# Results of the embedding stage's last three blocks in another part of the buffer, and the last norm of the output projection behind the first gate-up unit

## The chip, the cores and the metric

The program runs on all 8 cores of one Trainium2 chip. The cores do not talk to each other: each takes one prompt of 2048 tokens and 128 sample tokens through the whole layer. The metric is the device time of the slowest core in microseconds (us). A core's TensorE (PE) multiplies, VectorE (DVE) and ScalarE (ACT) do the elementwise work, GpSimd (POOL) issues the weight loads and SyncE (SP) issues the other transfers.

## What is computed

One layer of a decoder, in bf16 matmuls and float32 elementwise work. Cut to what matters:

```
h = x + 0.5 * rmsnorm(swiglu(rmsnorm(x) , W1))                 # FFN 1
n = rmsnorm(h) ; b,c,h_a,u,v = n @ W_in                        # mixer
y_a = b * causal_conv3(c * h_a) ; y_b = u * (tril(W_s) @ rmsnorm(v) + b_s)
h = h + rmsnorm(concat(rmsnorm(y_a), rmsnorm(y_b)) @ W_out)    # output projection
h = h + 0.5 * rmsnorm(swiglu(rmsnorm(h), W2))                  # FFN 2
h = h + rmsnorm(sigmoid(h @ W_pg) * (p @ W_pp))                # embedding stage
swiglu(x) = (silu(x @ W_gate) * (x @ W_up)) @ W_down
```

The model width is 1024, the hidden width of an FFN 2816 (22 column blocks of 128).

## The kernel before

A core works in two **passes**. Pass 0 has nine blocks of 128 tokens in three tiles of 384, pass 1 has eight blocks in two tiles of 512. Each pass runs these stages: gate-up of FFN 1 (`gu_stage`), down projection (`tok_stage`), `mixer`, output projection (`tok_stage` again, with lag 3), gate-up of FFN 2, down projection, and the embedding stage (`ple`). There is no scheduler: each engine executes its instructions in the order in which this Python code issues them, and waits on semaphores where `wait` puts them.

**A gate-up unit** (`gu_unit`) is two hidden blocks j of one tile: for each, 8 matmuls of the gate and 8 of the up part into a PSUM bank each. ACT takes Silu of the gate bank into one of two `sg` buffers, DVE multiplies the up bank with it into `hmid` (the product). There are eight banks, taken in rotation, so the ninth group of matmuls needs the first bank back. The first three weight slots (`heads`) are used on all tiles in turn: units (0,0), (1,0), (2,0) of tile 0, then (0,1), (1,1), (2,1) of tile 1, and so on. A hook can be issued inside a unit: `(s, ti): (jj, fn)` issues fn behind product jj of unit (s, ti).

**The output projection** makes, for each block b, one pair of banks. ACT takes the square sum, Ln and Exp of it (`post_stat`), DVE updates `h` (`post_apply`). The norm ahead of FFN 2 lags a block behind (`pend` and `pre_fn`): ACT squares `h` into one of two `nbr` buffers, then Ln and Exp, then DVE scales it into `nbr`, and SP issues a transpose DMA into `nT` (`pre_mid`, `pre`, `turn`). Two transposes are never in flight at once. A buffer's next Square waits until its transpose has landed. The last block's norm is issued at the end of `tok_stage`, ahead of everything of the gate-up stage. Then SP issues two gain loads, POOL the load of p (`pT`), and `pay_owed` lets POOL issue the weight fills that `hold_fills` held back, once the last transpose has landed.

**The buffer `big`** holds, one after the other, `hmid` of a pass, the mixer's work, and in the embedding stage the results `gb(b)` of its blocks. Counted in float32 columns, `hmid` block j lies at 576 j. Before the change `gb(b)` of blocks 0 to 3 lies at 1024 b, of blocks 4 and 5 in `zsc`, and blocks 6, 7 and 8 use the places of blocks 0, 1 and 2 again. The first x tile of pass 1 lies at 8192 to 12287, the second at 4096 to 8191. The embedding stage works in groups of three blocks. It also normalises the first x tile of pass 1 (`x_apply`) in group 1; the second is squared and normalised from the hooks `next_square` and `next_mid` in pass 1's gate-up.

Each result is stored to HBM by SP (`store`, event `out_ev[b]`). `gb_guard` lets a block's Sigmoid wait for what was in its place; `guard1` does the same for the products of pass 1's first gate-up.

Of the kernel before, what the change touches and what calls it, by code (L numbers as in the profile page):

```python
# [26 lines left out]
G1POST, GMPRE, GMPOST, G2PRE, G2POST, GPLE = range(6)  # L27
NGAIN = 6
# [92 lines left out]
def build_program():  # L121
    nc = bass.Bass("TRN2", target_bir_lowering=False)
# [9 lines left out]
    pT_d = din("pT", [128, 2, NTOK])  # L132
# [19 lines left out]
    POOL = Eng(nc, nc.gpsimd, "pool")  # L152

    h_t = nc.alloc_sbuf_tensor("h", [128, 9, D], F32)
    nT_t = nc.alloc_sbuf_tensor("nT", [128, 8, WMAX], BF16)
# [3 lines left out]
    zsc_t = nc.alloc_sbuf_tensor("zsc", [128, 2, D], F32)  # L159
# [13 lines left out]
    bigf = big_t[:].bitcast(F32)  # L173
# [5 lines left out]
        return hmid[:, j0:j0 + 8, b * 128:(b + 1) * 128]  # L179

    def gb(b):
        i = b % 6
        return zsc_t[:, i - 4, :] if i >= 4 else bigf[:, 1024 * i:1024 * (i + 1)]

    ps = [nc.alloc_psum_tensor("ps%d" % i, [128, 1024], F32) for i in range(4)]
    banks = [Bank(ps[i // 2][:, 512 * (i % 2):512 * (i % 2) + 512]) for i in range(8)]
# [73 lines left out]
    def pay_owed(wait, limit=2 * NFILL):  # L260
        POOL.wait(wait)
        wr["limit"] = limit
        n, wr["owed"] = wr["owed"], 0
        for _ in range(n):
            issue_next()
# [17 lines left out]
    def gain_load(i, wait=None):  # L283
        if i >= 2 * NGAIN:
            return
        SP.wait(wait)
        gain_ev[i] = gain_sem[i % 3].add(nc.sync.dma_start(
            out=gain_t[:, i % 3, :], in_=gain_d[i % NGAIN:i % NGAIN + 1, :].broadcast_to([128, D])))
# [22 lines left out]
    nT_ev = {}  # L311
# [141 lines left out]
    def gu_stage(P, heads, guard, hooks=None, order=None):  # L453
        hooks = hooks or {}
        hd = [next_fill() for _ in range(heads)]
        evl = None
        nt = len(P.tiles)
        for s, ti in order or [(s, ti) for ti in range(nt) for s in range(heads)]:
            f, fev = hd[s]
            evl = gu_unit(P, f, fev, 2 * s, ti, guard, hooks.get((s, ti)))  # L460
            if ti == nt - 1:
                release(f, evl)
        for s in range(heads, NFF // 2):
            f, fev = next_fill()
            for ti in range(nt):
                evl = gu_unit(P, f, fev, 2 * s, ti, guard, hooks.get((s, ti)))
            release(f, evl)


    xn_ev = {}  # L470
# [89 lines left out]
    def tok_stage(P, nk, nfl, lhs, wait, gpost, c, lag, j0, pre_fn, hooks=None):  # L560
        fl = [next_fill() for _ in range(nfl)]
        pend = None
        for b in range(P.nb):
            last = b == P.nb - 1
            pair, ev = proj_block(P, b, nk, lambda k, b=b: lhs(b, k), 4, fl, wait(b), last)
            if hooks and b in hooks:
                hooks[b](ev)
            st = post_stat(b, pair, ev, c, j0)
            e = post_apply(b, pair, st, gpost)
            if lag == 1:  # L570
                pre_fn(b, ev)
            else:
                if pend is not None:
                    pre_fn(*pend)
                pend = (b, ev)
        if pend is not None:
            pre_fn(*pend)
        return e


    vo_sem = DmaSem(nc, "vo")
# [389 lines left out]
    h_free = {}  # L971

    def gb_guard(b):
        return [guards["zsc"] if b % 6 >= 4 else None, out_ev.get(b - 6) if b >= 6 else None]


    first = x_stat(PASSES[0], 0, x_square(PASSES[0], 0))
# [33 lines left out]
    for P in PASSES:  # L1011
        base = P.idx * NGAIN
        N = PASSES[P.idx + 1] if P.idx == 0 else None

        def guard1(j, P=P):
            if P.idx == 0:
                return None
            lo, hi = j * 576 // 1024, (j * 576 + 575) // 1024
            evs = [out_ev.get(x + 6 if x < 3 else x) for x in range(lo, hi + 1) if x < 4]
            if hi >= 4:  # L1020
                evs += [xn_ev[1, 1][-1], xn_ev[1, 0][-1]]
            return evs

        def guard_none(j):
            return None

        if P.idx == 0:
            gu_stage(P, 2, guard1, {(1, 0): (1, start_square), (1, 1): (0, start_mid), (2, 0): (0, start_loads),
                                    (8, 0): (0, late_consts)},
                     [(0, 0), (0, 1), (1, 0), (1, 1), (0, 2), (1, 2)])  # L1030
        else:
            gu_stage(P, 3, guard1, {(0, 0): (1, next_square), (1, 0): (1, next_mid)})
        xn_ev.clear()
        def pre_mid(gi):
            def f(b, ev_d):
                dst, ev_t = turn_buffer()
                last_pre["ev"] = e = pre(b, gi, dst, [ev_d, ev_t])
                turn(b, dst, e)
            return f

        last_pre = {"ev": None}
        nT_ev.clear()
        hold_fills()
        tok_stage(P, NFF, 6, lambda b, k: hmid[:, k, b * 128:(b + 1) * 128], lambda b, P=P: [hm[P.tile_of(b)]],
                  base + G1POST, 4.0, 1, 14, pre_mid(base + GMPRE))
        pay_owed([nT_ev[P.nb - 1]])
        gain_load(base + G2PRE, [last_pre["ev"]])
        gain_load(base + G2POST, [last_pre["ev"]])

        norm_ev, tail, vo_last = mixer(P)  # L1050
        ACT.wait(vo_last)
        nT_ev.clear()
        tok_stage(P, 8, 2, lambda b, k: nT_t[:, k, b * 128:(b + 1) * 128], lambda b: [norm_ev[b]],
                  base + GMPOST, 1.0, 3, 0, pre_mid(base + G2PRE), {0: tail})
        gain_load(base + GPLE, [last_pre["ev"]])
        gain_load(base + NGAIN + G1POST, [last_pre["ev"]])

        POOL.wait(vo_last, last_pre["ev"])
        w = P.tiles[-1][0] + P.tiles[-1][1]
        pT_ev = None  # L1060
        for i, r0 in enumerate(sorted(set([P.rows[0]] + ([P.rows[8]] if P.nb == 9 else [])))):
            n = 1024 if i == 0 else 128
            pT_ev = pt_sem.add(nc.gpsimd.dma_start(out=pT_v[:, :, i * 1024:i * 1024 + n], in_=pT_d[:, :, r0:r0 + n]))
        pay_owed([nT_ev[P.nb - 1]])
        gu_stage(P, 3, guard_none)
        hold_fills(1)

        def next_x(ev):
            xt_load(PASSES[1], 0, 1, [ev])

        def cast(b, ev_d):
            dst, ev_t = turn_buffer()
            turn(b, dst, copy_v([h_ev[b], ev_t], dst, h_t[:, b, :].rearrange("p (k s) -> p k s", k=8)))

        nT_ev.clear()
        tok_stage(P, NFF, 6, lambda b, k: hmid[:, k, b * 128:(b + 1) * 128], lambda b, P=P: [hm[P.tile_of(b)]],
                  base + G2POST, 4.0, 1, 0, cast, {8: next_x} if N is not None else None)
        guards["zsc"] = h_ev[P.nb - 1]
        groups = [[0, 1, 2], [3, 4, 5], [6, 7, 8]] if P.nb == 9 else [[0, 1, 2], [3, 4, 5], [6, 7]]
        ple(P, N, base, pT_ev, groups)  # L1080
        if N is not None:
            pay_owed([xt_ev[1, 1]])
        zfree[0], zfree[1] = out_ev[4], out_ev[5]
# [101 lines left out]
```

How the kernel before makes its waits and increments, by code:

```python
    def wait(self, *evs):  # L62
        best = {}
        for ev in _flat(evs, []):
            if ev.key not in best or best[ev.key].val < ev.val:
                best[ev.key] = ev
        for ev in best.values():
            if self.seen.get(ev.key, 0) >= ev.val:
                continue
            self.e.wait_ge(ev.sem, ev.val)
            self.seen[ev.key] = ev.val
            if _COLLECT is not None and ev.idx is not None:
                _COLLECT.add((ev.key, ev.idx))
# [1 line left out]
    def mark(self, ins):  # L75
        self.idx += 1
        if _USED is not None and (self.name, self.idx) not in _USED:
            return Ev(self.sem, self.n, self.name, self.idx)
        self.n += 1
        ins.then_inc(self.sem, 1)
        return Ev(self.sem, self.n, self.name, self.idx)
# [8 lines left out]
    def add(self, ins):  # L90
        self.n += 16
        ins.then_inc(self.sem, 16)
        return Ev(self.sem, self.n, self.name)
```

## Time and profile before

| quantity | before |
|---|---|
| time, median of 3 runs | 1333.33 us (1333.08 to 1335.34) |
| time of the profiled execution | 1332.94 us |
| its span on the slowest core (core 2) | 1331.8 us |
| spans of the eight cores | 1326.5 to 1331.8 us |
| PE busy in the span | 1290.0 us (97%) |
| mean granted TensorE clock, by core | 0.989 to 0.993 |
| a weight transfer of 512 KB, from issue to landing (median) | 15.1 us |
| table loads on ACT (core 2) | 25 |

The profile's rows come from one profiled execution. A timeline row has the start in us from the span's start, the length in us, the engine and line, the operation as output<-inputs with the shape, and how many instructions it merges. In brackets stands the idle time ahead of it and what ended it. Some matmul records are missing, so a merged row can show 63 where 64 ran.

### The profile page before, as it was taken

How to read it: one execution, taken by the hardware profiler on the slowest of the kernel's cores; microseconds unless marked ns; L12 is line 12 of the kernel's file. 1: busy time of each engine (PE TensorE's matmuls, PEld its weight loads, DVE VectorE, ACT ScalarE, POOL GpSimd, SP SyncE). 2: the span in 40 equal slices, each digit the busy share in tenths (PEclk: the TensorE clock that was granted, in tenths of full speed). 3: DMA queues.
4: the chain of work that ended last, by engine and by line, in shares of the span. 5: the costliest groups of instructions: out<-in, count | busy, mean ns of one | idle time of the engine just before them, and what ended most of it. 6: DMA issues, size and time to landing. Idle time of an engine off the chain costs nothing.

```text
span 1331.8 us, 18723 instructions; the slowest of 8 cores (1326.5 to 1331.8 us)
## 1 busy us (share of the span) xinstructions
PE 1290.0 (97%) x6734; PEld 651.8 (49%) x6816; DVE 524.1 (39%) x694; ACT 411.3 (31%) x862; POOL 94.7 (7%) x185
## 2 busy tenths in 40 slices
PE   8999999999999999999998999999999999999995
PEld 6566664455545666654443344444444444444442
DVE  3222222447696222213266321223477922122237
ACT  3311112344465111111166211123334721111136
POOL 2110000001001100000001100000010011000000
PEclk9999999999999999999999899999999999999998
DMA  8999322129725963231289994332297299333123
GB/s 186 201 208 207 65 48 48 24 39 178 123 49 108 168 110 64 48 72 25 48 176 257 215 182 79 58 62 32 48 179 130 56 144 175 69 63 58 32 40 126
DMA packets 88906, 139.89 MB, mean 105 GB/s; under 512 B 58352, under 2 KB 58608, under 8 KB 88432
## 3 DMA queue, kind: packets, MB, share of 16 engines
q0 software_dynamic: 25296, 90.25, 41.1%
q1 hardware_dynamic: 63520, 48.43, 13.5%
q8 instruction: 57, 0.93, 0.3%
q14 instruction: 33, 0.27, 0.1%
HBM read 206.03 MB, written 9.51 MB: 162 GB/s over the span
## 4 chain that ended last, share of the span: by engine, by line
PE 85%; DVE 5%; ACT 4%; DMA 3%; issue 3%; SPq 0%; ACTq 0%; DVEq 0%
PE ps L212 56%; PE ps L557 24%; PE ps L546 3%; DVE nT L221 1%; DMA y<-big 1%; DMA nT<-nbr 1%; ACT big L217 1%; DMA h<-xT 1%; DVE big L225 1%; DVE big L221 1%; ACT sg L217 1%; DVE nbr L221 1%; ACT L217 1%; PE ps L711 1%; ACT nbr L217 1%
## 5 line engine op out<-in xcount | busy, mean ns | idle before, releaser
L212 PE MATMUL ps<-nT,ring 128*128 128x384 bf16 (+1 forms) x4127 | 776.6, 349 | 16.4 <-DVE nT L221 7.9
L212 PEld LDWEIGHTS ps<-nT,ring 128*128 128x128 bf16 x4160 | 407.9, 98 | 381.4 <-issue 29.4
L225 DVE TENSOR_TENSOR big<-ps,sg 128x384 bf16<-128x384 f32 (+1 forms) x220 | 134.0, 611 | 489.3 <-PE ps L212 469.8
L557 PE MATMUL ps<-ring,big 128*128 128x512 bf16 x1291 | 283.7, 379 | 1.5
L217 ACT ACTIVATE sg<-ps 128x384 f32<-128x384 f32 (+1 forms) x237 | 127.0, 537 | 500.9 <-PE ps L212 490.3
L557 PEld LDWEIGHTS ps<-ring,big 128*128 128x128 bf16 x1320 | 129.2, 98 | 155.5
L253 POOL DMA_DIRECT2D ring<-w x170 | 90.2, 539 | 1066.7 <-PE ps L212 461.5
L217 ACT ACTIVATE big<-ps 128x1024 bf16<-128x1024 f32 (+4 forms) x89 | 75.4, 862 | 226.3 <-PE ps L557 195.2
L225 DVE TENSOR_TENSOR zsc<-ps,gains 128x1024 f32<-128x1024 f32 x51 | 62.3, 1222 | 180.2 <-ACT big L217 180.1
L557 PE MATMUL ps<-ring,nT 128*128 128x512 bf16 x470 | 104.9, 379 | 2.1 <-DVE big L225 1.4
L557 PEld LDWEIGHTS ps<-ring,nT 128*128 128x128 bf16 x480 | 46.8, 98 | 58.3 <-issue 2.5
L221 DVE SCALAR_TENSOR_TENSOR h<-zsc,st,h 128x1024 f32<-128x1024 f32 x51 | 65.5, 1285 | 11.1 <-DVE zsc L225 6.7
L225 DVE TENSOR_TENSOR big<-ps,big 128x384 f32<-128x384 f32 (+3 forms) x78 | 50.3, 678 | 39.8 <-PE ps L212 20.4
L221 DVE SCALAR_TENSOR_TENSOR nbr<-h,st,gains 128x1024 bf16<-128x1024 f32 x34 | 43.6, 1282 | 36.4 <-ACT st L217 36.4
L217 ACT ACTIVATE nbr<-h 128x1024 bf16<-128x1024 f32 x34 | 35.9, 1057 | 50.4 <-DVE h L221 41.9
L217 ACT ACTIVATE st<-st 128x1 f32<-128x1 f32 x205 | 41.7, 203 | 18.7 <-ACT st L217 0.7
L546 PE MATMUL ps<-ring,big 128*128 128x512 bf16 x175 | 38.6, 379 | 0.1
L217 ACT ACTIVATE big<-big 128x384 bf16<-128x384 f32 (+3 forms) x46 | 26.2, 605 | 38.0 <-DVE big L225 38.0
L217 ACT ACT_TABLE_LOAD x25 | 32.1, 1283 | 13.0 <-PE ps L212 6.0
L212 PE MATMUL ps<-ring,nT 128*128 128x512 bf16 x131 | 29.4, 379 | 0.3
L546 PEld LDWEIGHTS ps<-ring,big 128*128 128x128 bf16 x176 | 17.2, 98 | 20.8
L221 DVE SCALAR_TENSOR_TENSOR big<-big,gc 128x384 f32<-128x384 f32 (+3 forms) x48 | 24.8, 590 | 0.0
(73 smaller groups left out, 363.5 us busy)
## 6 DMA issues: line engine op xcount, KB each, us to landing
ring<-w POOLq DMA_DIRECT2D x170, 512.0 KB, 15.1
h<-x SPq DMA_DIRECT2D x17, 512.0 KB, 30.2
gains<-gain SPq DMA_DIRECT2D x12, 512.0 KB, 9.2
y<-big SPq DMA_DIRECT2D x12, 512.0 KB, 10.8
big<-xT SPq DMA_DIRECT2D x2, 2048.0 KB, 13.8
y<-zsc SPq DMA_DIRECT2D x4, 512.0 KB, 6.2
h<-xT SPq DMA_DIRECT2D x4, 384.0 KB, 5.9
h<-xT SPq DMA_DIRECT2D x2, 768.0 KB, 10.7
```

Of the source, the lines that this page charges most:

```text
L212: ins = nc.tensor.matmul(out_ap, l, r, start=(i == 0), stop=(i == n - 1))
L217: return ACT.mark(nc.scalar.activation(**kw))
L221: return DVE.mark(nc.vector.scalar_tensor_tensor(out=out, in0=in0, scalar=scalar, in1=in1, op0=op0, op1=op1))
L225: return DVE.mark(nc.vector.tensor_tensor(out=out, in0=in0, in1=in1, op=op))
L253: nc.gpsimd.dma_start(out=ring_t[:, s, o:o + HALF], in_=w_d[f % NFILL, :, o:o + HALF])))
L546: ins = nc.tensor.matmul(o.t, lhs(k), sv[:, k % per, half * 512:half * 512 + 512], start=(k == 0), stop=(k == nk - 1))
L557: ins = nc.tensor.matmul(o.t, lhs(k), sv, start=(k == 0), stop=(k == nk - 1))
L711: ins = nc.tensor.matmul(bank.t[:, 0:w], ones_t[:], sq[i][:, 0:w], start=(c == 0), stop=(c == 3))
```

## The change

Two things are changed. First, `gb(b)` of blocks 6, 7 and 8 lies at 8192, 9216 and 10240, in the room of pass 1's first x tile. Their Sigmoid waits until that tile has been normalised, where it waited for the stores of blocks 0, 1 and 2. The products of pass 1's first gate-up wait for the stores of whatever lies in their place now: blocks 0 to 3 for the first places, blocks 6 to 8 from place 8192 on. Second, `tok_stage` returns its pending block instead of issuing its norm. After the output projection that norm, and all that came behind it (two gain loads, the load of p, the held fills), is issued as a hook behind the second product of unit (0,0).

```diff
@@ gb @@
-        i = b % 6
-        return zsc_t[:, i - 4, :] if i >= 4 else bigf[:, 1024 * i:1024 * (i + 1)]
+        if b in (4, 5):
+            return zsc_t[:, b - 4, :]
+        o = 1024 * b if b < 4 else 8192 + 1024 * (b - 6)
+        return bigf[:, o:o + 1024]
@@ tok_stage @@
-        if pend is not None:
-            pre_fn(*pend)
-        return e
+        return pend
@@ gb_guard @@
-        return [guards["zsc"] if b % 6 >= 4 else None, out_ev.get(b - 6) if b >= 6 else None]
+        if b in (4, 5):
+            return [guards["zsc"]]
+        return [xn_ev[1, 0][-1]] if b >= 6 and (1, 0) in xn_ev else []
@@ guard1 @@
-            evs = [out_ev.get(x + 6 if x < 3 else x) for x in range(lo, hi + 1) if x < 4]
-            if hi >= 4:
-                evs += [xn_ev[1, 1][-1], xn_ev[1, 0][-1]]
+            evs = []
+            for x in range(lo, hi + 1):
+                if x < 4:
+                    evs.append(out_ev[x])
+                elif x < 8:
+                    evs.append(xn_ev[1, 1][-1])
+                else:
+                    evs += [xn_ev[1, 0][-1], out_ev[x - 2] if x < 11 else None]
@@ the pass loop @@
-        tok_stage(P, 8, 2, lambda b, k: nT_t[:, k, b * 128:(b + 1) * 128], lambda b: [norm_ev[b]],
-                  base + GMPOST, 1.0, 3, 0, pre_mid(base + G2PRE), {0: tail})
-        gain_load(base + GPLE, [last_pre["ev"]])
-        gain_load(base + NGAIN + G1POST, [last_pre["ev"]])
-
-        POOL.wait(vo_last, last_pre["ev"])
...
-        pay_owed([nT_ev[P.nb - 1]])
-        gu_stage(P, 3, guard_none)
+        pre_ffn2 = pre_mid(base + G2PRE)
+        pend = tok_stage(P, 8, 2, lambda b, k: nT_t[:, k, b * 128:(b + 1) * 128], lambda b: [norm_ev[b]],
+                         base + GMPOST, 1.0, 3, 0, pre_ffn2, {0: tail})
+        ple_in = {}
+
+        def last_norm(P=P):
+            pre_ffn2(*pend)
+            gain_load(base + GPLE, [last_pre["ev"]])
+            gain_load(base + NGAIN + G1POST, [last_pre["ev"]])
+            POOL.wait(vo_last, last_pre["ev"])
...
+            pay_owed([nT_ev[P.nb - 1]])
+
+        gu_stage(P, 3, guard_none, {(0, 0): (1, last_norm)})
```

What stands on DVE where pass 0 ends and pass 1 begins: the last block of the embedding stage, then the products of pass 1's first gate-up (`big<-ps,sg`), then the normalising of the second x tile (`nT<-big,gc,ps`). y6 is the store of block 6. Before:

```order
L221 SCALAR_TENSOR_TENSOR big<-big,st,gains 128x1024 [waits sem_act]
L225 TENSOR_TENSOR big<-big,h 128x1024 [waits sem_dve]
L225 TENSOR_TENSOR big<-ps,sg 128x512 [waits sem_act,sem_pe,y6]
L225 TENSOR_TENSOR big<-ps,sg 128x512 [waits sem_act,sem_pe,y7]
L225 TENSOR_TENSOR big<-ps,sg 128x512 [waits sem_act,sem_pe]
L225 TENSOR_TENSOR big<-ps,sg 128x512 [waits sem_act,sem_pe,y8]
L221 SCALAR_TENSOR_TENSOR nT<-big,gc,ps 128x512 [waits sem_act]
L221 SCALAR_TENSOR_TENSOR nT<-big,gc,ps 128x512 x7
```

The same place after:

```order
L223 SCALAR_TENSOR_TENSOR big<-big,st,gains 128x1024 [waits sem_act]
L227 TENSOR_TENSOR big<-big,h 128x1024 [waits sem_dve]
L227 TENSOR_TENSOR big<-ps,sg 128x512 [waits sem_act,sem_pe,y0]
L227 TENSOR_TENSOR big<-ps,sg 128x512 [waits sem_act,sem_pe,y1]
L227 TENSOR_TENSOR big<-ps,sg 128x512 [waits sem_act,sem_pe]
L227 TENSOR_TENSOR big<-ps,sg 128x512 [waits sem_act,sem_pe,y2]
L223 SCALAR_TENSOR_TENSOR nT<-big,gc,ps 128x512 [waits sem_act]
L223 SCALAR_TENSOR_TENSOR nT<-big,gc,ps 128x512 x7
```

The instructions and their order are the same; the stores waited for are those of blocks 0, 1 and 2 where they were those of 6, 7 and 8.

What stands on ACT at the end of pass 1's output projection: `nbr,st<-h` is the Square of a block's norm, `st<-st` its Ln and Exp, `sg<-ps` a Silu of the gate-up stage; t0 and t1 are transposes. Before:

```order
L217 ACTIVATE st<-st 128x1 [waits sem_act] x2
L217 ACTIVATE nbr,st<-h 128x1024 [waits sem_dve,t1]
L217 ACTIVATE st<-st 128x1 [waits sem_act] x2
L217 ACTIVATE nbr,st<-h 128x1024 [waits sem_dve,t0]
L217 ACTIVATE st<-st 128x1 [waits sem_act] x2
L217 ACTIVATE sg<-ps 128x512 [waits sem_pe] x2
L217 ACTIVATE sg<-ps 128x512 [waits sem_pe,sem_dve] x42
```

The same place after:

```order
L219 ACTIVATE st<-st 128x1 [waits sem_act] x2
L219 ACTIVATE nbr,st<-h 128x1024 [waits sem_dve,t1]
L219 ACTIVATE st<-st 128x1 [waits sem_act] x2
L219 ACTIVATE sg<-ps 128x512 [waits sem_pe] x2
L219 ACTIVATE nbr,st<-h 128x1024 [waits sem_dve,t0]
L219 ACTIVATE st<-st 128x1 [waits sem_act] x2
L219 ACTIVATE sg<-ps 128x512 [waits sem_pe,sem_dve] x42
```

Two Silus moved ahead of the last block's Square, Ln and Exp. Pass 0 has the same move at its output projection. Table loads of ACT are not listed here; they come where the function changes between Silu and Ln or Exp.

## Rows read from the trace of the kernel before

**Rows 1.** The page: PE's share, and the chain that ended last by engine.

```profile
PE 1290.0 (97%) x6734; PEld 651.8 (49%) x6816; DVE 524.1 (39%) x694; ACT 411.3 (31%) x862; POOL 94.7 (7%) x185
...
PE 85%; DVE 5%; ACT 4%; DMA 3%; issue 3%; SPq 0%; ACTq 0%; DVEq 0%
```

**Rows 2.** Waits: who waited for whom, total us, times, longest.

```profile
DVE big L225 <- DMA y<-big: 13.5, 3, 5.6
...
PE ps L212 <- DVE nT L221: 7.9, 11, 3.7
```

**Rows 3.** Timeline of PE where pass 0 ends and pass 1 begins.

```profile
709.22 13.97 PE L212 MATMUL ps<-nT,ring 128*128 128x512 bf16 x63
723.03 1.89 PE L500 MATMUL ps<-nT,ones 128*128 128x512 bf16 x7
727.83 8.75 PE L212 MATMUL ps<-nT,ring 128*128 128x512 bf16 x32 [2.91 <-DVE big L225]
738.28 0.38 PE L212 MATMUL ps<-nT,ring 128*128 128x512 bf16 x1 [1.70 <-DVE nT L221]
```

**Rows 4.** Timeline of DVE in the same stretch.

```profile
720.10 1.22 DVE L225 TENSOR_TENSOR big<-big,h 128x1024 f32<-128x1024 f32 x1
726.89 0.69 DVE L225 TENSOR_TENSOR big<-ps,sg 128x512 bf16<-128x512 f32 x1 [5.57 <-DMA y<-big]
...
737.40 5.34 DVE L221 SCALAR_TENSOR_TENSOR nT<-big,gc,ps 128x512 bf16<-128x512 f32 x8
...
760.47 0.69 DVE L225 TENSOR_TENSOR big<-ps,sg 128x512 bf16<-128x512 f32 x1 [2.76 <-PE ps L212]
```

**Rows 5.** Timeline of ACT in the same stretch.

```profile
718.12 1.09 ACT L217 ACTIVATE sg<-ps 128x512 f32<-128x512 f32 x2
719.10 3.89 ACT L217 ACTIVATE nT<-big 128x1024 bf16<-128x1024 f32 x4
...
733.05 1.28 ACT L217 ACT_TABLE_LOAD   x1
734.34 1.25 ACT L217 ACTIVATE ps<-ps 128x512 f32<-128x512 f32 x2
```

**Rows 6.** Windows: busy time by engine, then granted clock, DMA share, GB/s.

```profile
736.00:745.00 9.00, 6.37 (x15) 1.62 (x15) 7.15 (x11) 2.69 (x4) 1.06 (x2) 0.68 1.03 176
```

**Rows 7.** Timeline of PE, pass 0, first gate-up units of FFN 2.

```profile
406.79 10.56 PE L212 MATMUL ps<-nT,ring 128*128 128x384 bf16 x64
419.17 41.11 PE L212 MATMUL ps<-nT,ring 128*128 128x384 bf16 x252 [1.82 <-ACT sg L217]
```

**Rows 8.** Timeline of ACT, pass 0: Ln and Exp of block 7's norm.

```profile
412.84 0.50 ACT L217 ACTIVATE st<-st 128x1 f32<-128x1 f32 x2
```

**Rows 9.** Timeline of ACT, pass 1: blocks 6 and 7 of the same norm.

```profile
1059.84 0.50 ACT L217 ACTIVATE st<-st 128x1 f32<-128x1 f32 x2
1062.00 1.06 ACT L217 ACTIVATE nbr<-h 128x1024 bf16<-128x1024 f32 x1 [1.66 <-DMA nT<-nbr]
```

**Rows 10.** Core 2, pass 1: PE's gate-up; the last two transposes; time to landing.

```profile
1054.51 40.74 PE L212 MATMUL ps<-nT,ring 128*128 128x512 bf16 x185 [1.15 <-DMA nT<-nbr]
...
1062.66 4.35 SPq L325 DMA_TRANSPOSE nT<-nbr  x2
...
DMA to landing us min/median/max: 3.0/3.0/7.6
```

**Rows 11.** Core 7, the same three.

```profile
1054.34 25.84 PE L212 MATMUL ps<-nT,ring 128*128 128x512 bf16 x119 [1.15 <-DMA nT<-nbr]
...
1062.51 4.34 SPq L325 DMA_TRANSPOSE nT<-nbr  x2
...
DMA to landing us min/median/max: 3.0/5.9/8.7
```

**Rows 12.** Core 7, start of pass 1: PE's first row, DVE's fifth product of tile 1.

```profile
708.74 13.97 PE L212 MATMUL ps<-nT,ring 128*128 128x512 bf16 x64
...
760.31 0.69 DVE L225 TENSOR_TENSOR big<-ps,sg 128x512 bf16<-128x512 f32 x1 [2.76 <-PE ps L212]
```

More of the change, by code:

```diff
@@ L1052, in build_program @@
         nT_ev.clear()
-        tok_stage(P, 8, 2, lambda b, k: nT_t[:, k, b * 128:(b + 1) * 128], lambda b: [norm_ev[b]],
-                  base + GMPOST, 1.0, 3, 0, pre_mid(base + G2PRE), {0: tail})
-        gain_load(base + GPLE, [last_pre["ev"]])
-        gain_load(base + NGAIN + G1POST, [last_pre["ev"]])
-        POOL.wait(vo_last, last_pre["ev"])
[L1059 to L1063, printed above, removed]
-        pay_owed([nT_ev[P.nb - 1]])
-        gu_stage(P, 3, guard_none)
+        pre_ffn2 = pre_mid(base + G2PRE)
[7 more added lines that the diff above has]
+            POOL.wait(vo_last, last_pre["ev"])
+            for i, r0 in enumerate(sorted(set([P.rows[0]] + ([P.rows[8]] if P.nb == 9 else [])))):
+                n = 1024 if i == 0 else 128
+                ple_in["ev"] = pt_sem.add(nc.gpsimd.dma_start(out=pT_v[:, :, i * 1024:i * 1024 + n],
+                                                              in_=pT_d[:, :, r0:r0 + n]))
+            pay_owed([nT_ev[P.nb - 1]])
+        gu_stage(P, 3, guard_none, {(0, 0): (1, last_norm)})
+        pT_ev = ple_in["ev"]
         hold_fills(1)
```

## The prediction

> **What bounds the kernel now.** I read the page first. PE is busy for 97% of the span and makes 85% of the chain that ended last [rows 1], so a time can only be won where PE stands still or runs at a lower clock. The list of waits says where that is. PE's largest wait is 7.9 us for DVE's normalising into nT, and DVE's one wait on a transfer in a PE-bound stretch is 13.5 us for stores `y<-big`, in three pieces [rows 2]. The timelines put both at the same place, the start of pass 1. I then read the other two places that the change touches: the output projections of both passes.
>
> **Part 1, the boundary of the passes.** In the first gate-up of pass 1 the first product on DVE could start when DVE is done with the last embedding block (720.10 + 1.22 = 721.3), but starts at 726.89, after 5.57 us of waiting for a store [rows 4]; the second and third pieces of the 13.5 us follow behind the next products. The products free PSUM banks and `sg` buffers, so PE stops for 2.91 us after the statistics matmuls, and again ahead of tile 1, where nT is normalised only from 737.40 on, one k every 0.67 us, each matmul waiting for one [rows 3, 4]. The standing PE also loses its clock: 0.68 of full speed in 736 to 745 [rows 6].
>
> What would PE do without any of this? 64 matmuls took 13.97 us, a last one included that takes 0.38, so the pace is (13.97 - 0.38) / 63 = 0.2157 us [rows 3]. The fifth product of tile 1, at 760.47 [rows 4], follows the 184th matmul from 709.22 (64, then 8 of the statistics, 32 of unit (2,0), and 80 of tile 1). Unhindered, that one ends at 709.22 + 183 x 0.2157 + 0.38 = 749.1, and the product starts about 0.1 later. So at most 760.47 - 749.2 = **11.3 us** are to be won here, clock included.
>
> Is all of it won? The stores now waited for, of blocks 0 to 2, were issued in group 0 of the embedding stage, more than 20 us earlier, so that wait is gone. What is late next is the way over ACT and DVE to the second x tile. ACT does its two Silus at 718.12 and the four squares until 719.10 + 3.89 = 723.0 [rows 5]. Then two more Silus (1.1, to 724.1, their buffers free since the products of 721.3 to 722.7), a table load of 1.28 (to 725.4), Ln and Exp of 1.25 (to 726.7) [rows 5]. The statistics matmuls end at 723.03 + 1.89 = 724.9 [rows 3], before that. DVE then needs 5.34 for the eight k [rows 4], so it ends at 732.1. PE does unit (2,0) from 724.8 to 731.7 (32 x 0.2157) and wants k = 7 of tile 1 at 731.7 + 7 x 0.2157 = 733.2. The margin is 1.1 us, so nothing of the wait comes back. If the chain were later than this, every us beyond 1.1 would be lost. The weights are there: PE waits for none in this stretch, and their loads go on as before. Moving the blocks' results costs nothing else. The Sigmoid of block 6 waits for the normalising of the first x tile instead of for a store, and DVE does that normalising before it does the products of group 1, whose statistics stand ahead of this Sigmoid on ACT. In pass 1 nothing of this kind was on the way.
>
> **Part 2, pass 0's output projection.** PE does the 64 matmuls of two units from 406.79 at a pace of (10.56 - 0.33) / 63 = 0.1624, could begin the ninth group at 417.18, and begins at 419.17, released by a Silu [rows 7]. That Silu stood behind block 8's norm, which waited for its buffer. After the change it stands behind block 7's Exp, which ends at 412.84 + 0.50 = 413.3 [rows 8], plus a table load of 1.28: it starts at 414.6, and its bank is free at 415.1, two us before it is wanted. **2.0 us** are won. The last norm then needs a table load more, is 1.5 us later, and the third Silu follows at about 420.0. Its bank is wanted at 417.2 + 32 x 0.1624 = 422.4, so PE does not stop again. Block 8 belongs to tile 2, which PE reaches after twelve j of 2.6 us, at 438; its transpose is issued at about 420.6 and, even with the 8.7 us of the slowest one shown [rows 11], is there by 429.3.
>
> **Part 3, pass 1's output projection.** Here PE did not wait for a Silu, so nothing is won. But the norm of block 7 gets later, and block 7 belongs to tile 1. Before: Square at 1062.00 [rows 9]. After: Exp of block 6 ends at 1059.84 + 0.50 = 1060.3, table load 1.28, two Silus 1.1, Square at 1062.7, 0.7 later; then one more table load of 1.28 ahead of Ln. Together the transpose is issued 2.0 us later. On core 2 the last transpose was issued at 1062.66 + 4.35 - 1.24 = 1065.8 and took 7.6 us (the load of p is issued with it, and stays with it), so it landed at 1073.4. PE wants tile 1 at 1054.51 + 96 x 0.2157 = 1075.2 [rows 10]. After: 1075.4, and 0.1 for PE to start: PE stands for **0.3 us**. On core 7 the same reckoning gives a landing at 1065.6 + 8.7 = 1074.3 against a want of 1075.05 [rows 11], so 1.3 us late afterwards: 1.3 us, 1.4 with the start. Cores with 1326 to 1330 us have larger margins or do not matter. The held fills start 2 us later too; the first of them is used after three heads and one more slot, at 1054.5 + 256 x 0.2157 = 1109.7, more than 30 us after its issue, and such a transfer takes 15 us.
>
> Here a rule speaks against the change. The rows show a switch of table as 1.28 us and nothing more: the load starts at 733.05 as the Silu ends, and Ln starts at 734.34 [rows 5]. The Trainium skill, "ScalarE: Activation LUTs", section "What ACT_TABLE_LOAD costs", adds a drain of about 1.38 us to each load of 1.28. By it the two switches ahead of the last norm would cost 2.8 us more. The sum below takes the row.
>
> **The sum.** Core 2: 1331.8 - 11.3 - 2.0 + 0.3 = 1318.8. Core 7 had 1331.6, and its stretch at the boundary, counted in the same way, holds 760.31 - 708.74 - 40.0 = 11.6 [rows 12]: 1331.6 - 11.6 - 2.0 + 1.4 = 1319.4. The slowest core ends at about 1319.2, that is 12.6 less. The profiled execution took 1332.94, the median is 0.4 above it; 1333.33 - 12.6 = **1320.7 us**.
>
> **Rivals.**
> (a) The boundary keeps a part: the way over squares, table load, Ln, Exp and eight normalising steps is 2 to 5 us longer than I built it, so that 1 to 4 us of the 11.3 stay, or PE's clock falls there all the same. For: it has six links and a margin of 1.1. Against: each link has a row. Time 1322 to 1325.
> (b) Each switch between Silu and Ln costs more than its row while other work is in ACT's pipe, 1.4 us a switch. Then block 7's transpose lands 2.8 us later still and PE stands 3.1 us (core 2) to 4.2 (core 7): 1323.5. Against: the rows show back-to-back starts on both sides of the load. This is the page's case, too.
> (c) The change does not do what it says at the boundary: another transfer, such as the stores of blocks 1 and 2, holds the products. These would have to be 20 us and more in flight; the longest wait for stores shown is for ones issued at 716 to 721. Then only part 2 remains: 1331.7.
> (d) The other side: in pass 1 the transpose of block 7, now issued as PE is in the middle of tile 0, lands far later than 7.6 us, because its slot among the load of p and the gain load is worse. It costs nothing up to 1.8 us of delay on core 2 and then us for us. To make the kernel slower by 0.2% it has to be 1.8 + 13.3 + 2.7 = 18 us later than before; 2 are worked out. Its price is then 1336 or more.
>
> **How the numbers follow.** The forecast as summed 0.80 (1319.0 to 1322.3 by the spread of the cores' terms: 11.0 to 11.9 at the boundary, 0 to 1.4 in part 3, and the spread of the runs), (a) 0.12, (b) 0.04, (c) 0.03, (d) 0.01. The range reaches over (b) and most of (a): 1319.0 to 1324.0. A measurement of this kernel tells about 0.2%, 2.7 us, from no change. Faster by more: 0.96; within: 0.03, from (c); slower: 0.01, from (d).
>
> **What would show it.** DVE's first product of pass 1 starts at the end of the last embedding block, with no idle time charged to `y<-big`; the row of 2.91 us and the seven of 0.28 us on PE are gone, and the clock is 1.00 in every window of the boundary. In pass 0 PE's row after 64 matmuls of FFN 2's gate-up has no wait for ACT. In pass 1 a new row of PE, 96 matmuls after the start of that gate-up, waits 0 to 1.5 us for `nT<-nbr`. ACT has two table loads more in each pass, 29 for 25. I am wrong if PE still stands at the start of tile 1 in pass 1's first gate-up, or if the new wait exceeds 2 us.

## The result, and the profile after

| quantity | before | after |
|---|---|---|
| time, median | 1333.9 us (4 runs, 1333.1 to 1335.3) | 1320.0 us (4 runs, 1319.7 to 1321.7) |
| profiled execution | 1332.94 us | 1319.69 us |
| its span, slowest core (core 2 in both) | 1331.8 us | 1318.6 us |
| spans of the eight cores | 1326.5 to 1331.8 us | 1314.7 to 1318.6 us |
| sum of PE's waits (core 2) | 22.2 us | 14.8 us |

The ratio is 0.9897, with a 95% interval of 0.988 to 0.9914. The medians here and below leave out the runs in which the cores of a die show a lower granted clock and a longer time (of after one in five, 1433.9 us).

The page of after: its span, the busy times, the chain that ended last, and the group of table loads.

```profile
span 1318.6 us, 18725 instructions; the slowest of 8 cores (1314.7 to 1318.6 us)
...
PE 1284.3 (97%) x6734; PEld 651.3 (49%) x6816; DVE 524.0 (40%) x694; ACT 415.6 (32%) x866; POOL 94.7 (7%) x185
...
PE 90%; DVE 3%; ACT 3%; issue 2%; DMA 2%; SPq 0%; ACTq 0%; DVEq 0%; POOLq 0%
...
L219 ACT ACT_TABLE_LOAD x29 | 37.2, 1283 | 13.6 <-PE ps L214 5.4
```

PE's busy time fell by 5.7 us with the same number of matmuls as in [rows 1]: that is clock won back. The rest of the 13.2 us is standing time. PE's part of the chain rose from 85% to 90%. The table loads are 29, as worked out.

PE's waits in after (who waited for whom, total us, times, longest):

```profile
PE ps L214 <- DMA ring<-w: 3.3, 1, 3.3
PE ps L214 <- DVE nT L223: 1.9, 7, 0.7
```

The first is PE's wait for the first weights at the start of the kernel. The second was 7.9 us in [rows 2], but less of that lay at the boundary than it seems. In the execution before, this row of PE's timeline stands at the kernel's start:

```profile
22.12 20.04 PE L212 MATMUL ps<-nT,ring 128*128 128x384 bf16 x112 [3.71 <-DVE nT L221]
```

This start wait (3.71 us) is still there after, 3.34 us at 21.84, now put down to the weights. Another 1.9 us, at 46 to 50 us, are the 1.9 of the second row. Only 2.3 us of the 7.9 were at the boundary, and these are gone. DVE's 13.5 us for `y<-big` is gone from the list too.

**The boundary of the passes.** PE of core 2, the stretch of [rows 3]:

```profile
707.09 13.97 PE L214 MATMUL ps<-nT,ring 128*128 128x512 bf16 x63
720.90 1.89 PE L502 MATMUL ps<-nT,ones 128*128 128x512 bf16 x7
722.62 42.68 PE L214 MATMUL ps<-nT,ring 128*128 128x512 bf16 x193
```

DVE in the same stretch, to be laid beside [rows 4]:

```profile
717.96 1.23 DVE L227 TENSOR_TENSOR big<-big,h 128x1024 f32<-128x1024 f32 x1
719.10 1.28 DVE L227 TENSOR_TENSOR big<-ps,sg 128x512 bf16<-128x512 f32 x2
721.51 1.29 DVE L227 TENSOR_TENSOR big<-ps,sg 128x512 bf16<-128x512 f32 x2 [1.13 <-ACT sg L219]
725.52 5.36 DVE L223 SCALAR_TENSOR_TENSOR nT<-big,gc,ps 128x512 bf16<-128x512 f32 x8 [2.72 <-ACT ps L219]
...
747.07 0.69 DVE L227 TENSOR_TENSOR big<-ps,sg 128x512 bf16<-128x512 f32 x1 [2.76 <-PE ps L214]
```

PE runs through without one idle stretch. The first product follows the last embedding block at once. The fifth product of tile 1 comes 747.07 - 707.09 = 39.98 us after PE's first matmul of the pass, where it took 51.25 before. The granted clock is full where it was 0.68 [rows 6] (columns: stretch, length, busy time of PE, weight load, DVE, ACT, POOL, then clock, DMA share, GB/s):

```profile
727.00:736.00 9.00, 8.95 (x42) 4.05 (x42) 5.77 (x9) 2.12 (x4) 1.06 (x2) 1.00 1.00 190
736.00:745.00 9.00, 8.95 (x42) 4.12 (x42) 2.08 (x3) 1.19 (x2) 1.06 (x2) 1.00 1.03 198
```

ACT in that stretch, beside [rows 5]:

```profile
720.75 1.08 ACT L219 ACTIVATE sg<-ps 128x512 f32<-128x512 f32 x2
722.87 1.28 ACT L219 ACT_TABLE_LOAD   x1 [1.04 <-PE ps L502]
724.16 1.26 ACT L219 ACTIVATE ps<-ps 128x512 f32<-128x512 f32 x2
```

Here one thing is not as worked out. The table load does not begin when the Silus end (721.8) but only at 722.87, after PE's statistics matmuls, for which the Ln behind it waits.

**Pass 0's output projection.** PE's timeline, where [rows 7] had a stop of 1.82 us:

```profile
406.62 23.56 PE L214 MATMUL ps<-nT,ring 128*128 128x384 bf16 x144
```

ACT's timeline there, to be laid beside [rows 8]:

```profile
413.20 1.28 ACT L219 ACT_TABLE_LOAD   x1
414.49 0.87 ACT L219 ACTIVATE sg<-ps 128x384 f32<-128x384 f32 x2
415.25 1.06 ACT L219 ACTIVATE nbr<-h 128x1024 bf16<-128x1024 f32 x1
...
419.58 0.87 ACT L219 ACTIVATE sg<-ps 128x384 f32<-128x384 f32 x2
```

From there to the first matmul of pass 1 the core took 709.22 - 406.79 = 302.43 us before and 707.09 - 406.62 = 300.47 after: 1.96 us less.

**Pass 1's output projection.** PE's timeline on core 2, the stretch of [rows 10]:

```profile
1041.12 39.23 PE L214 MATMUL ps<-nT,ring 128*128 128x512 bf16 x178 [1.16 <-DMA nT<-nbr]
```

ACT's, the stretch of [rows 9]:

```profile
1047.11 1.28 ACT L219 ACT_TABLE_LOAD   x1
1048.41 1.08 ACT L219 ACTIVATE sg<-ps 128x512 f32<-128x512 f32 x2
1049.38 1.06 ACT L219 ACTIVATE nbr<-h 128x1024 bf16<-128x1024 f32 x1
...
1050.60 1.28 ACT L219 ACT_TABLE_LOAD   x1
1051.90 0.50 ACT L219 ACTIVATE st<-st 128x1 f32<-128x1 f32 x2
```

DVE's row of block 7's scaling:

```profile
1052.50 1.28 DVE L223 SCALAR_TENSOR_TENSOR nbr<-h,st,gains 128x1024 bf16<-128x1024 f32 x1 [2.03 <-ACT st L219]
```

SyncE's row of block 7's transpose (start, length and number), and its time to landing:

```profile
L327 SPq DMA_TRANSPOSE nT<-nbr x1: 1232/1232/1232, 1053.9 to 1053.9; - x1
...
DMA to landing us min/median/max: 7.3/7.3/7.3
```

The transpose lands at 1053.9 + 7.3 = 1061.2, and PE wants tile 1 at 1041.12 + 96 x 0.2157 = 1061.8. Core 2 does not wait, and in this execution neither does any other.

### The profile page after: what moved, and what is told of

Its sections match the earlier page's. It is cut to its first block, busy times and chain, and to the rows that moved or that the text cites. A ratio compares the mean times of both kernels' runs of the same rounds, so it can differ in the third digit from the quotient of the medians.

```text
span 1318.6 us, 18725 instructions; the slowest of 8 cores (1314.7 to 1318.6 us)
## 1 busy us (share of the span) xinstructions
PE 1284.3 (97%) x6734; PEld 651.3 (49%) x6816; DVE 524.0 (40%) x694; ACT 415.6 (32%) x866; POOL 94.7 (7%) x185
## 4 chain that ended last, share of the span: by engine, by line
PE 90%; DVE 3%; ACT 3%; issue 2%; DMA 2%; SPq 0%; ACTq 0%; DVEq 0%; POOLq 0%
PE ps L214 59%; PE ps L559 26%; PE ps L548 3%; DVE nT L223 1%; DMA h<-xT 1%; DVE big L223 1%; ACT sg L219 1%; ACT big L219 1%; DVE big L227 1%; ACT L219 1%; DMA ring<-w 1%; PE ps L711 1%; DMA nT<-nbr 0%; PE ps L862 0%; PE ps L807 0%
## 5 line engine op out<-in xcount | busy, mean ns | idle before, releaser
L214 PEld LDWEIGHTS ps<-nT,ring 128*128 128x128 bf16 x4160 | 407.5, 98 | 368.3 <-issue 13.5
L219 ACT ACT_TABLE_LOAD x29 | 37.2, 1283 | 13.6 <-PE ps L214 5.4
L223 DVE SCALAR_TENSOR_TENSOR nT<-big,gc,zsc 128x384 bf16<-128x384 f32 (+1 forms) x40 | 23.9, 667 | 2.2 <-ACT zsc L219 2.2
## 6 DMA issues: line engine op xcount, KB each, us to landing
ring<-w POOLq DMA_DIRECT2D x170, 512.0 KB, 14.8
```

The lines of the kernel that those rows point to most:

```text
L214: ins = nc.tensor.matmul(out_ap, l, r, start=(i == 0), stop=(i == n - 1))
L219: return ACT.mark(nc.scalar.activation(**kw))
L223: return DVE.mark(nc.vector.scalar_tensor_tensor(out=out, in0=in0, scalar=scalar, in1=in1, op0=op0, op1=op1))
```

## Experiments

Two theories stood against each other at the boundary. **Theory W:** DVE's waits for late stores cost the 11.3 us, and their way goes over PE's banks, the second x tile and the clock. **Theory P:** it is not these waits but something else that went with them, the places in the buffer or the norm's order. For the norm, theory N said that pass 0 gains 2 us and pass 1 pays 0 to 1.4 us for a later transpose. The diffs are against after.

The cores reach one and the same instruction at times that differ by some us from core to core and from execution to execution. So the table has, beside the median, the time from PE's first matmul of FFN 2's gate-up in pass 0 (406.62 on core 2 of after) to the core's end, lowest and highest of the eight cores of the profiled execution. All that the experiments touch lies in this stretch. It was 924.7 to 926.1 us before and 911.7 to 912.2 after.

| run | what | median, us | ratio to before (95%) | gate-up to end, us |
|---|---|---|---|---|
| e1_place_only | norm where it was | 1323.1 | 0.9917 (0.9901 to 0.9934) | 913.6 to 913.7 |
| e2_norm_only | places and waits of before | 1330.8 | 0.9977 (0.9966 to 0.9987) | 921.3 to 922.5 |
| e3_old_waits | places of after, waits of before as well | 1331.4 | 0.9979 (0.9966 to 0.9991) | 921.6 to 924.1 |
| e4_one_wait | only the first of these waits | 1326.6 | 0.9941 (0.9925 to 0.9958) | 914.2 to 918.7 |
| e5_norm_later | pass 1: norm one unit later | 1325.9 | 0.9939 (0.9923 to 0.9955) | 913.9 to 917.9 |
| e6_norm_pass0 | norm moved in pass 0 alone | 1321.3 | 0.9908 (0.9892 to 0.9923) | 911.6 to 912.2 |
| e7_two_copies | 3.9 us of spare work ahead of Ln | 1323.4 | 0.9928 (0.9914 to 0.9942) | 914.4 to 914.6 |
| e8_early_load | table load pulled ahead | 1320.1 | 0.9902 (0.9886 to 0.9918) | 911.6 to 912.2, one core 913.4 |
| e9_later_p_after | e5, load of p behind the transpose | 1321.3 | 0.991 (0.9894 to 0.9927) | 911.6 to 911.9 |
| e10_later_both_after | e9, gain loads behind it too | 1319.7 | 0.9898 (0.9883 to 0.9913) | 911.7 to 912.2 |
| e11_both_after | after, both loads behind, and e8 | 1319.8 | 0.9898 (0.9882 to 0.9915) | 911.6 to 912.0 |

### Each half alone

e1_place_only issues the norm ahead of the gate-up stage again:

```diff
-        gu_stage(P, 3, guard_none, {(0, 0): (1, last_norm)})
+        last_norm()
+        gu_stage(P, 3, guard_none)
```

> The changed kernel with the last norm of the output projection issued where the kernel before had it; only the place of the results of blocks 6 to 8 and the waits that follow from it are new. My theory: the 11.3 us of the boundary of the passes (waits on stores, waits on x tile 2, lower clock) are all this part's, so 11 to 11.5 us less than before, some 1322.5; PE in pass 0 waits 1.8 us for a Silu again. Rival, the two parts work together (the boundary is won only with the norm moved): well under 11 us.

The boundary took 750.78 - 710.80 = 39.98 us on the slowest core (core 7), so all of the 11.3 us is there without the norm's move. In pass 0 PE's wait was back (its timeline):

```profile
420.75 3.57 PE L214 MATMUL ps<-nT,ring 128*128 128x384 bf16 x21 [1.85 <-ACT sg L219]
```

The median is 3.1 us above after's. The wait accounts for 1.7 to 1.8 of it: from the start of the gate-up in pass 0 to the end the core took 1322.0 - 408.33 = 913.7 us, against 1318.6 - 406.62 = 912.0, and the other seven cores agree. In the profiled executions the rest, 408.33 - 406.62 = 1.7 us, is how late the slowest core came to that gate-up; of this more below.

e2_norm_only has `gb`, `gb_guard` and `guard1` of before and the norm of after:

```diff
@@ gb @@
...
+        i = b % 6
+        return zsc_t[:, i - 4, :] if i >= 4 else bigf[:, 1024 * i:1024 * (i + 1)]
...
@@ guard1 @@
...
+            evs = [out_ev.get(x + 6 if x < 3 else x) for x in range(lo, hi + 1) if x < 4]
...
```

> The kernel before with only the last norm moved behind the first gate-up unit. My theory: 2.0 us less than before (pass 0's wait of 1.8 us for a Silu goes), nothing or up to 0.5 us lost in pass 1, so some 1331.5 to 1332; the boundary of the passes is as before, with three waits on stores of 13 us in total. Rival, each switch of ACT's table costs 1.4 us more than its row: Ln of the last norm starts 2.7 us after its table load begins and pass 1 shows a wait of PE for a transpose of 2 us and more, so no gain.

It gained 3.1 us, a little more than expected. DVE waited for stores again at the boundary (6.47, 4.29 and 2.90 us on core 6), which lost 758.61 - 707.78 - 39.98 = 10.85 us. In pass 1 no core waited for the later transpose. The two halves are independent as far as this tells: what each is worth alone (10.8 and 3.1 by the medians) adds up to the whole, 13.9.

### The waits, not the places

e3_old_waits keeps every place of after and adds waits that nothing needs, for the stores of blocks 6, 7 and 8:

```diff
                 if x < 4:
                     evs.append(out_ev[x])
+                    evs.append(out_ev[x + 6] if x < 3 else None)
```

> The changed kernel, with the new places, but the products of pass 1's first gate-up wait for the stores of blocks 6, 7 and 8 as well, as they did before (nothing needs these waits now). My theory: the wait alone is the cost, so the 11.3 us come back: 2 us less than before, some 1332. Rival, the gain comes from the places (transfers or engines meeting in the same part of the buffer): most of the 11 us stays won, some 1321 to 1323.

DVE on the slowest core (core 0):

```profile
724.64 0.69 DVE L227 TENSOR_TENSOR big<-ps,sg 128x512 bf16<-128x512 f32 x1 [5.83 <-DMA y<-big]
729.52 1.29 DVE L227 TENSOR_TENSOR big<-ps,sg 128x512 bf16<-128x512 f32 x2 [4.18 <-DMA y<-big]
734.20 0.69 DVE L227 TENSOR_TENSOR big<-ps,sg 128x512 bf16<-128x512 f32 x1 [3.40 <-DMA y<-big]
...
758.83 0.69 DVE L227 TENSOR_TENSOR big<-ps,sg 128x512 bf16<-128x512 f32 x1 [2.76 <-PE ps L214]
```

This is the picture of [rows 4], and with PE's first matmul at 706.71 the fifth product came 52.1 us later, 12.1 more than in after. The median is 11.4 us above after's. On the eight cores the stretch from the gate-up to the end is 10 to 12 us longer than in after. Theory W holds, and P falls: the new places are worth nothing but the waits that they make needless.

e4_one_wait adds the first of the three waits only:

```diff
+                    evs.append(out_ev[6] if x == 0 else None)
```

> The changed kernel, but the first product of pass 1 waits for the store of block 6 too; those of blocks 7 and 8 are not waited for. My theory: product 0 starts about 5.5 us late, the banks and the second x tile follow: PE stands 2.9 us ahead of unit (2,0) and up to 1 us at tile 1, and the clock falls for some us: 4 to 5.5 us slower than the changed kernel, some 1325 to 1326. Rival, the three waits add up only by the last one (block 8), the first being covered by the banks in hand: within 1 us of the changed kernel. If the clock does not fall after 2.9 us of standing, 3 to 4 us.

DVE's timeline on the slowest core (core 4):

```profile
727.50 1.29 DVE L227 TENSOR_TENSOR big<-ps,sg 128x512 bf16<-128x512 f32 x2 [6.23 <-DMA y<-big]
```

PE's, on the same core:

```profile
728.45 36.77 PE L214 MATMUL ps<-nT,ring 128*128 128x512 bf16 x163 [3.57 <-DVE big L227]
```

One window of it, columns as above:

```profile
727.00:736.00 9.00, 7.55 (x29) 3.15 (x30) 6.49 (x10) 6.12 (x8) 0.77 (x3) 0.81 1.03 254
```

The stretch took 754.31 - 709.17 = 45.14 us, 5.16 more than in after: 3.57 of standing, and the other 1.6 of clock, which was 0.81 in the window with the end of the stop and what follows it. On this core one wait of 6.2 us on DVE thus costs 5.2; over the eight cores waits of 4.3 to 7.3 us cost 2.3 to 6.8 (by the stretch to the end, against some 911.9). With the other two waits the cost is 10 to 12. The median is 6.6 us above after's, more than the 4 to 5.5 expected; the slowest core had again come late to pass 0's gate-up (408.72 against 406.62).

### How much room the second x tile has

e7_two_copies puts two spare copies on ACT ahead of the statistics' Ln (the result is not touched):

```diff
     def next_mid():
+        e = None
+        for _ in range(2):
+            e = act([e, t_ev], out=nbr_t[:].rearrange("p i k s -> p (i k s)"), in_=XT[1, 1][:, 0:2048], func=AF.Copy)
```

> The changed kernel with 3.8 us of spare work on ACT (two copies of 2048 columns into an idle buffer) between the Silus of unit (1,0) and the Ln of the second x tile's statistics. If ACT's table load ahead of that Ln waits until the statistics are done, as the row of the changed kernel looks (load at 722.87, after 1.04 us of waiting for PE), the load moves from 722.87 to 725.7: Ln and all behind it 2.8 us later, the margin of 0.15 us at k = 7 used up, PE loses 2.7 us and maybe some clock: some 1323.5. If the margin is the 1.1 us of my prediction, PE loses 1.7 us. Rival, the way over ACT has slack that the rows do not show: no loss.

ACT's timeline on the slowest core (core 4):

```profile
723.41 3.92 ACT L219 ACTIVATE nbr<-big 128x2048 bf16<-128x2048 f32 x2
727.34 1.28 ACT L219 ACT_TABLE_LOAD   x1
```

DVE's, on the same core:

```profile
730.00 5.35 DVE L223 SCALAR_TENSOR_TENSOR nT<-big,gc,ps 128x512 bf16<-128x512 f32 x8 [5.48 <-ACT ps L219]
...
737.71 0.69 DVE L227 TENSOR_TENSOR big<-ps,sg 128x512 bf16<-128x512 f32 x1 [1.16 <-PE ps L214]
```

The first of PE's six stops there:

```profile
732.20 0.38 PE L214 MATMUL ps<-nT,ring 128*128 128x512 bf16 x1 [0.28 <-DVE nT L223]
```

The normalising started 730.00 - 708.80 = 21.20 us after PE's first matmul, against 725.52 - 707.09 = 18.43 in after: 2.77 later. The first product of tile 1 came 737.71 - 708.80 = 28.91 us after it, where after (at 733.25) took 26.16: 2.75 later. So nearly all of the delay reached PE, and every core shows it: the stretch to the end is 2.5 to 2.7 us longer than the 911.9 that is the middle of after's. With the margin of 1.1 us that the prediction gave to this way, 1.7 would have reached PE.

e8_early_load lets ACT compute one column's Ln that waits for nothing, ahead of the Ln of the statistics:

```diff
     def next_mid():
+        act([ev_ones], out=st_t[:, 15, 3:4], in_=ones_t[:, 0:1], func=AF.Ln)
```

> The changed kernel with one spare Ln of one column ahead of the statistics' Ln, which waits for nothing, so that the table load is done while PE still makes the statistics. My theory: the Ln starts 0.8 to 0.9 us earlier, the normalising of the second x tile ends 0.8 us earlier and the margin at k = 7 grows from 0.15 to 1.0 us; the time is the same as the changed kernel's, since PE does not wait there. Rival, PE does wait there on some cores: up to 0.5 us faster.

ACT's timeline on the slowest core (core 0):

```profile
721.18 1.28 ACT L219 ACT_TABLE_LOAD   x1
722.48 0.20 ACT L219 ACTIVATE st<-ones 128x1 f32<-128x1 bf16 x1
```

DVE's normalising there:

```profile
723.95 5.36 DVE L223 SCALAR_TENSOR_TENSOR nT<-big,gc,ps 128x512 bf16<-128x512 f32 x8 [1.81 <-ACT ps L219]
```

The load now lies beside the statistics matmuls, and the normalising starts 723.95 - 706.42 = 17.53 us after PE's first matmul, 0.9 earlier than in after. So the missing 0.9 us of margin was the table load behind Ln's wait. The time is after's, since PE waited for nothing there in after. In the same execution core 0 waited for block 7's transpose in pass 1 (PE's timeline):

```profile
1062.82 17.43 PE L214 MATMUL ps<-nT,ring 128*128 128x512 bf16 x80 [1.49 <-DMA nT<-nbr]
```

It had taken 9.6 us to land. The norm is issued there as in after.

### The norm in pass 1, and what makes its transpose slow

e6_norm_pass0 moves the norm in pass 0 only:

```diff
+        if P.idx == 0:
+            gu_stage(P, 3, guard_none, {(0, 0): (1, last_norm)})
+        else:
+            last_norm()
+            gu_stage(P, 3, guard_none)
```

> The changed kernel with the last norm moved in pass 0 alone; pass 1 issues it as before. My theory: the move wins nothing in pass 1 and costs nothing there either now, so the same time as the changed kernel within 0.5 us (about 1320.5 to 1321). Rival, the move helps pass 1 too (Silus earlier): up to 2 us slower than the changed kernel. Rival, it costs pass 1 up to 1.4 us on the slowest core: 1319.5.

Its median is 1.3 us above after's, with runs from 1319.9 to 1321.4 us; by these the two can't be told apart. The stretch from the gate-up to the end is sharper: 911.6 to 912.2 us, as in after. Moving the norm in pass 1 neither wins nor loses in these executions.

e5_norm_later moves it one unit further there, `(P.idx, 0)` for `(0, 0)`:

> The changed kernel with pass 1's last norm issued behind the second gate-up unit instead of the first (pass 0 as changed). My theory: the transpose is issued some 4.3 us later (Square behind the Silu of block j = 3) and lands at about 1065.5 against PE's want of tile 1 at 1061.8: PE waits 3 to 4.5 us, the kernel is that much slower than the changed one, some 1324 to 1325; that shows how near the changed kernel is to paying. Rival, the transpose has no use for its time because PE is fed by other tiles: no wait, same time.

PE's timeline on the slowest core (core 0):

```profile
1067.70 12.64 PE L214 MATMUL ps<-nT,ring 128*128 128x512 bf16 x50 [3.82 <-DMA nT<-nbr]
```

Time from issue to landing of SyncE's transposes in that stretch:

```profile
DMA to landing us min/median/max: 3.0/3.0/7.2
```

All eight cores waited, 2.0 to 4.3 us, where 3 to 4.5 were expected. The last transposes took 5.4 to 7.7 us, though the same transfer takes 3.0 elsewhere. e9_later_p_after keeps the late norm and lets POOL start the load of p only when that transpose has landed:

```diff
-            POOL.wait(vo_last, last_pre["ev"])
+            POOL.wait(vo_last, last_pre["ev"], nT_ev[P.nb - 1])
```

> The kernel of e5_norm_later (pass 1's last norm behind the second unit), but POOL issues the load of p only when the last transpose has landed, in both passes. Open: why that transpose takes 5.4 to 7.7 us where the others take 3.0. My theory: it shares the DMA engines with the load of p issued at the same moment, so it lands in 3 to 4 us now, and the wait of PE for it falls from 2.0 to 4.3 us by core to about 0 to 1: some 1321.5. Rival, the gain load that SP issues behind it is as much in its way: landing and wait stay, some 1325. Rival, the cause is outside the core (memory traffic of the other cores): landing stays at 5 to 8.

Their time to landing on the slowest core (core 7):

```profile
DMA to landing us min/median/max: 3.0/3.0/3.1
```

It was 3.0 to 3.1 us on every core, and no core's PE waited: 4.6 us of e5's 5.9 came back. e10_later_both_after lets the gain loads wait as well (the second is issued behind the first on SyncE):

```diff
-            gain_load(base + GPLE, [last_pre["ev"]])
+            gain_load(base + GPLE, [last_pre["ev"], nT_ev[P.nb - 1]])
```

> As e9_later_p_after, and SP issues the gain loads too only when the last transpose has landed. If either load holds the transpose up, it lands in 3.0 to 3.1 us on every core and PE waits for it nowhere: 1320.5 to 1321. If the cause is outside the core, 5 to 8 us stay.

The landings were 3.0 to 3.1 us again, so the gain loads add nothing to the transpose's time. The load of p is what stretches it. The median is 1.6 us below e9's, but from the gate-up of pass 0 to the end the slowest cores of the two profiled executions took the same: 1319.3 - 407.62 = 911.7 and 1318.7 - 407.05 = 911.7 us. Nothing behind that point makes the difference.

e11_both_after is the candidate for a better kernel: after, with both loads behind the transpose and the early table load of e8.

> The changed kernel (norm behind the first unit) with the load of p and the gain loads behind the last transpose's landing, and with the early table load of e8. My theory: no core can wait for block 7's rows any more (one of eight did, 1.49 us, in e8's profiled execution), the margins at the boundary are 1 us; the time is that of the changed kernel or up to 0.7 us less, 1320 to 1321. Rival, the later loads of p and of the fills are missed somewhere: slower, above 1322.

No core waits for the last transpose, which lands in 3.0 to 3.2 us, and it takes 1319.8 us, which can't be told from after's 1320.0. No kernel here beats after by what can be measured.

## Why the prediction was right, point by point

**The forecast.** 1320.7 us against 1320.0, and 12.6 less in the profiled execution against 1332.94 - 1319.69 = 13.25. (By the medians the fall is 13.9, as that of before came out at 1333.9. The 12.6 goes with an end at 1319.2, where the line for core 7 gives 1319.4.) The sum of the two gains measured on core 2, 11.27 + 1.96 = 13.23, is its whole difference of 1331.8 - 1318.6 = 13.2.

**Part 1, 11.3 us: right, and for the reason given.** The pace of 0.2157 us laid over the 184 matmuls gave the 40.0 us of the free way. After and e1 show it, and in e3 the waits take it away again. The clock's part was rightly inside that count and not added to it. One reading was off: the whole 7.9 us for `nT` were put at the boundary and seven stops of 0.28 us there, where 2.3 us and two such stops are charged on core 2. The sum did not use them. PE's standing in the stretch adds up to 2.9 + 2.3 + 0.2 = 5.4 us, so more than half of the 11.3 was clock.

**The margin of 1.1 us: wrong in size.** The normalising ended at 725.52 + 5.36 = 730.88, and PE wanted the eighth k of tile 1 at 722.62 + 39 x 0.2157 = 731.03. That leaves 0.15 us. The step that failed is "a table load of 1.28 (to 725.4)". Counted from PE's first matmul of the pass, the two Silus were to end at 14.9 us and ended at 14.7, the statistics matmuls were to end at 15.7 and did. But the load was taken to start with the Silus' end and to run beside these matmuls, and it waited for them with its Ln: Ln was worked out for 725.4 - 709.22 = 16.2 us and came at 724.16 - 707.09 = 17.1. These 0.9 us are what e8 wins back. The result was right by 0.15 us, and e7 shows what more would have cost: us for us, though without the clock. That nothing at all was lost here was in part luck.

**Part 2, 2.0 us: right.** It came as 1.96, the Silu at 414.49 (worked out: 414.6), the third one at 419.58 (420.0).

**Part 3, a loss of 0.3 to 1.4 us: wrong, it was 0.** DVE's scaling came 2.05 us later, as worked out (1052.50 - 1041.12 = 11.38 us after the gate-up's start, against 1063.84 - 1054.51 = 9.33). The step that failed is the next one: "Together the transpose is issued 2.0 us later". In the execution before, DVE was done with the scaling at 1065.1:

```profile
1063.84 1.28 DVE L221 SCALAR_TENSOR_TENSOR nbr<-h,st,gains 128x1024 bf16<-128x1024 f32 x1 [1.30 <-ACT st L217]
```

The transpose was issued only at 1065.8, when the one ahead of it had landed (1062.66 + 3.0 = 1065.7), which I had not put into the sum. So it moved by 12.78 - 11.27 = 1.5 us only. The landing then took 7.3 us where 7.6 had been put in, and on the eight cores the longest lay between 5.5 and 7.9, against 6.7 to 8.7 before. Core 7, for which the sum had 1.4, lost nothing either: from the gate-up of pass 0 it took 1331.6 - 406.28 = 925.3 us before and 911.7 after, 13.6 less, which is 11.6 + 2.0. The term can still come: e8 shows 1.49 us on a core whose transpose took 9.6. In the profiled executions of after, e2, e3, e4, e7 and e8, with the norm issued alike, that is one core of 48.

**The rivals.** (a), a part of the boundary kept: no, but by 0.15 us and not by 1.1. (b), 1.4 us more for each table switch: no. Square and the read of its sum end at 1050.5, the load follows, Ln starts at 1051.90, and DVE's delay of 2.05 us is the 0.77 by which Square came later after the gate-up's start (8.26 against 7.49 us) and 1.28 for the load, with nothing left. By the Trainium skill, "ScalarE: Activation LUTs", section "What ACT_TABLE_LOAD costs", it would have been 1.4 us more; the trace differs, and the measurement decides. (c), other stores hold the products: no, `y<-big` holds DVE nowhere at the boundary. (d), the transpose so late that the kernel gets slower: no; the worst landing of this transpose in any profiled execution was 9.6 us, and even e5, a unit later, lost 5.9 us.

**What the sum had not foreseen.** Which core is slowest changes from execution to execution with how far each has come at the first gate-up of FFN 2: 401.8 to 406.8 us before, 403.0 to 406.6 after, 401.4 to 408.5 in e5. Most of this stands already about 40 us into the kernel, behind PE's waits for the first weights and the first x tiles: of the 7.1 us between the two extreme cores of e5, 6.3 are there at one matmul of the first gate-up (44.69 against 38.40 us). It is why the slowest cores of e1 and e5 ended 1.7 and 1.9 us further from after's than the stretch behind this point explains. For the unprofiled runs this is not shown, but it is a spread that medians of three to eight runs carry too.

## What to carry to other kernels

When a buffer is used again, look at which of its tenants leaves last, and give the first writer of the next stage a place whose tenant has long gone. A wait of 6 us on DVE that keeps PSUM banks can cost PE nearly as much, clock included (5.2 in e4), and three of them 11, while PE's own waits show about half of it (5.4 of 11.3 us on core 2 before the change).

Count the free way of the bound engine by its pace from one fixed instruction to another, ahead of the stall and behind it; that gives standing time and clock in one number. For a step that is moved, take its start as the latest of all that it waits for, the transfer ahead of it in the same queue included. A step can be late already for another reason, and then part of a delay costs nothing. And where cores start a stretch at different times, compare kernels by the time from one fixed instruction to the end: here it repeats within 0.6 us (911.6 to 912.2), where the medians of e9 and e10 lie 1.6 us apart.

## What the runs showed of the hardware

**A table load stands behind the wait of the instruction that needs it.** In after ACT idled 1.04 us and only then loaded (722.87), with the Silus done at 721.8. An activation of one column with no wait of its own, in e8, brought the load 0.9 us forward.

**A DMA transpose was slow beside one load and not beside another.** The same transpose (128x1024 bf16) took 3.0 to 3.1 us without the load of p (512 KB, started by POOL) and 5.4 to 7.7 us in e5 when that was issued with it (9.6 once, in e8). The order in time of the two settled it (e5 against e9). The gain loads (512 KB each, from SyncE, issued right behind the transpose) did not matter (e9 against e10). Why the one stretches it and the others do not is not shown.

**Long stops cost clock, shorter ones and pacing did not.** The granted clock was 0.81 in the window around the end of a stop of 3.57 us (e4), which cost 1.6 us on top. Seven of e4's cores stopped there once, for 2.07 to 4.67 us, and each shows a lower clock behind it; the eighth, with a stop of 1.62 and two of 0.19 and 0.28 us, kept 1.00. So did all eight cores before the change around the stop of 1.8 us in pass 0. The clock stayed at 1.00 on every core of e7 too, where PE stood 0.28 us ahead of each of six matmuls (727 to 736 on core 4):

```profile
727.00:736.00 9.00, 7.31 (x31) 2.82 (x30) 6.00 (x10) 5.15 (x7) 0.33 (x1) 1.00 1.02 220
```

Before the change, where both came together (2.91 and 1.70 us of standing and then the paced matmuls), it was 0.68 [rows 3, 6].

**The same work took the same time on every core.** From the gate-up of FFN 2 in pass 0 to the end, all 47 cores without an extra wait in the profiled executions of after, e6, e8, e9, e10 and e11 took 911.6 to 912.2 us, though they came to it between 401.7 and 408.5.
